# A triangular inverse on one NeuronCore: identity folded into its factors, the products copied by ScalarE, and the second token tile's products written to the other half of the partitions

## The reference, cut to what matters

```python
def gated_delta_rule(q, k, v, g, beta):          # 8 heads, chunks of 64 tokens
    ...
    a_mat = jnp.where(strict, jnp.einsum('nbhid,nbhjd->nbhij', kb, kc) * decay, 0.0)
    t_mat = a_mat + jnp.eye(CHUNK, dtype=jnp.float32)
    rhs = jnp.concatenate([vc * bc[..., None], kb * jnp.exp(gc)[..., None]], axis=-1)
    sol = lax.linalg.triangular_solve(t_mat, rhs, left_side=True, lower=True, unit_diagonal=True)
```

## Time and profile before

| what | value |
|---|---|
| time of three runs | median 2469.0 us (2468.1 to 2474.7) |
| the profiled execution | 2470.6 us, of which 2468.8 us are the span of the trace |
| TensorE | busy 2403.3 us, 97% of the span |
| VectorE | busy 1501.5 us, 61% |
| ScalarE | busy 1068.1 us, 43% |
| GpSimd | busy 151.8 us, 6% |

### The profile page before, as it was taken

One profiled execution on the slowest core, in us unless ns is written; L12 is line 12 of the kernel. 1 busy time (PEld: TensorE's weight loads), 2 busy tenths in 40 slices (PEclk: granted clock), 3 DMA queues, 4 the chain that ended last, 5 costly groups with the idle time before them and its releaser, 6 DMA issues. The chain is left out here.

```text
span 2468.8 us, 42893 instructions
## 1 busy us (share of the span) xinstructions
PE 2403.3 (97%) x18882; PEld 2222.7 (90%) x18882; DVE 1501.5 (61%) x2042; ACT 1068.1 (43%) x1319; POOL 151.8 (6%) x177
## 2 busy tenths in 40 slices
PE   8999999999999999999999999999998999999998
PEld 8999889999999799899889989899997998998997
DVE  5457664465567645667565556755676556866554
ACT  4334643333336543363343345533465335533432
POOL 0100000020000100001110000100001000111000
PEclk9999999999999999999999999999999999999999
DMA  6756355575564455543155554555545555423553
GB/s 228 241 188 155 107 175 184 186 226 190 185 165 128 151 187 186 158 139 104 53 196 188 188 156 137 171 188 188 178 137 171 188 188 162 121 87 103 181 188 118
DMA packets 320809, 405.37 MB, mean 164 GB/s; under 512 B 48688, under 2 KB 281232, under 8 KB 320624
## 3 DMA queue, kind: packets, MB, share of 16 engines
q1 hardware_dynamic: 314960, 383.50, 49.1%
q0 software_dynamic: 5664, 19.13, 2.5%
HBM read 401.55 MB, written 1.05 MB: 163 GB/s over the span
## 5 line engine op out<-in xcount | busy, mean ns | idle before, releaser
L402 DVE TENSOR_TENSOR w_lo<-raw,w_hi 128x2048 fp32r<-128x2048 f32 (+2 forms) x363 | 813.6, 2266 | 123.7 <-ACT w_hi L395 123.4
L395 ACT CAST w_hi<-raw 128x2048 fp32r<-128x2048 f32 (+2 forms) x363 | 685.5, 1890 | 462.5 <-PE ps L410 403.8
L408 PE MATMUL ps<-aT_hi,w_hi 128*128 128x256 f32 x2840 | 810.3, 285 | 0.0
L409 PE MATMUL ps<-aT_lo,w_hi 128*128 128x256 f32 x2840 | 804.4, 283 | 0.0
L410 PE MATMUL ps<-aT_hi,w_lo 128*128 128x256 f32 x2840 | 804.3, 283 | 0.0
L408 PEld LDWEIGHTS ps<-aT_hi,w_hi 128*128 128x128 f32 x2840 | 543.3, 191 | 7.0 <-issue 1.9
L409 PEld LDWEIGHTS ps<-aT_lo,w_hi 128*128 128x128 f32 x2840 | 543.5, 191 | 4.2 <-issue 0.5
L410 PEld LDWEIGHTS ps<-aT_hi,w_lo 128*128 128x128 f32 x2840 | 543.3, 191 | 0.5
L408 PE MATMUL ps<-w_hi,h_hi 128*128 128x512 f32 x928 | 363.6, 392 | 5.8 <-DVE h_lo L1758 4.6
L409 PE MATMUL ps<-w_lo,h_hi 128*128 128x512 f32 x928 | 362.6, 391 | 0.0
L410 PE MATMUL ps<-w_hi,h_lo 128*128 128x512 f32 x928 | 361.4, 389 | 0.0
(11 more groups left out here) (370 smaller groups left out, 1944.6 us busy)
## 6 DMA issues: line engine op xcount, KB each, us to landing
raw<-in_mlp_w SPq DMA_DIRECT2D x128, 1024.0 KB, 5.4
raw<-in_ffn_wd SPq DMA_DIRECT2D x44, 1024.0 KB, 4.9
raw<-in_ffn_wg SPq DMA_DIRECT2D x43, 1024.0 KB, 5.3
raw<-in_ffn_wu SPq DMA_DIRECT2D x43, 1024.0 KB, 5.3
raw<-in_gdn_w_in SPq DMA_DIRECT2D x32, 1024.0 KB, 5.7
raw<-in_mlstm_w_in SPq DMA_DIRECT2D x12, 1024.0 KB, 5.4
raw<-in_diff_w_in SPq DMA_DIRECT2D x12, 1024.0 KB, 5.3
raw<-in_w_in SPq DMA_DIRECT2D x8, 1024.0 KB, 5.2
```

Source lines behind the costliest of these rows:

```text
L395: nc.scalar.copy(used_part(hi_slot(n), n), used_part(raw[:, n % RAW, :], n)).then_inc(hi_ready, 1)
L402: nc.vector.tensor_tensor(used_part(lo_slot(n), n), used_part(raw[:, n % RAW, :], n), used_part(hi_slot(n), n).bitcast(F32), ALU.subtract) ...
L408: nc.tensor.matmul(dst, l_hi, r_hi, start=start, stop=False)
L409: nc.tensor.matmul(dst, l_hi, r_lo, start=False, stop=False)
```

## The change

The matrices are stored with the identity folded in: the masks of a level become "identity plus mask", and A becomes I - A, so that `right_set` yields I - Y, and the products T (I - Y) and (I - Y)T are the new T and its transpose without a subtraction. VectorE's `inverse_set` is gone; ScalarE copies the products from PSUM in `inverse_copied`. In `const_gdn` the diagonal is taken out of the chunk mask that spreads the row factors. `first_level` ends with a product by the mask in two halves for the second tile, since its transposed T is stored with the two chunks' partitions exchanged.

`blocks`, one call for each token tile, is replaced by `quarters`, one call for both: for each head it issues tile 0 chunk 0, tile 0 chunk 1, tile 1 chunk 0, tile 1 chunk 1. Where `over[t]` is set the output goes to the other half of the partitions. It is set for the second tile in `right`, in the first product of `both`, in the product by the identity at u = 10 and in the last level's second product; for levels 1 to 4 the second product of `both` has it unset for both tiles. One signal follows a call, and TensorE waits for both tiles ahead of it.

```diff
-    gdn = np.concatenate([same, np.where(col >= row, 0.0, NEG), row == col, level(0, col, row)]
-                         + [level(v, row, col) for v in range(1, LEVELS)], 1)
+    unit = (row == col).astype(np.float32)
+    gdn = np.concatenate([same & (s != t), np.where(col >= row, 0.0, NEG), unit, unit + level(0, col, row)]
+                         + [unit + level(v, row, col) for v in range(1, LEVELS)], 1)
...
-        def blocks(bank, lhs, rhs):
-
-            for h in range(HN):
-                for r in CK:
-                    last = nc.tensor.matmul(ps[r, bank, CHUNK * h:CHUNK * h + CHUNK], lhs[r, h, :], rhs(r, h), start=True, stop=True)
-            return last
...
+        def quarters(banks, lhs, rhs, over):
+
+
+            for h in range(HN):
+                for t in range(TT):
+                    for q, r in enumerate(CK):
+                        o = CK[1 - q] if over[t] else r
+                        last = nc.tensor.matmul(ps[o, banks[t], CHUNK * h:CHUNK * h + CHUNK], lhs[r, t, h, :], rhs(r, t, h),
+                                                start=True, stop=True)
+            return last
+
         def right(v):
             for t in range(TT):
                 if v == 1:
                     done(gd_T0, t)
                 else:
                     done(inv_t, TT * (v - 1) + t)
-                blocks(4 + t, g_A[:, t, :, :], lambda r, h: g_T[r, t, h, :]).then_inc(inv_y.sem, 1)
+            quarters((4, 5), g_A, lambda r, t, h: g_T[r, t, h, :], (0, 1)).then_inc(inv_y.sem, 1)
 
         def both(v):
             for t in range(TT):
                 done(inv_ys, TT * (v - 1) + t)
-                if v < LEVELS - 1:
-                    blocks(4 + t, g_TT[:, t, :, :], lambda r, h: g_Y[r, t, h, :])
-                blocks(6 + t, g_Y[:, t, :, :], lambda r, h: g_TT[r, t, h, :]).then_inc(inv_z.sem, 1)
+            if v < LEVELS - 1:
+                quarters((4, 5), g_TT, lambda r, t, h: g_Y[r, t, h, :], (0, 1))
+            quarters((6, 7), g_Y, lambda r, t, h: g_TT[r, t, h, :], (0, v == LEVELS - 1)).then_inc(inv_z.sem, 1)
...
             if u == 10:
                 for t in range(TT):
                     done(inv_t, t)
-                    blocks(4 + t, g_TT[:, t, :, :], lambda r, h: id64[r, :]).then_inc(inv_y.sem, 1)
+                quarters((4, 5), g_TT, lambda r, t, h: id64[r, :], (0, 1)).then_inc(inv_y.sem, 1)
...
+        def inverse_copied(v):
+            for t in range(TT):
+                done(inv_z, v - 1)
+                if v < LEVELS - 1:
+                    nc.scalar.copy(g_T[:, t, :, :], ps[:, 4 + t, :].rearrange("p (h c) -> p h c", c=CHUNK))
+                nc.scalar.copy(g_TT[:, t, :, :], ps[:, 6 + t, :].rearrange("p (h c) -> p h c", c=CHUNK)).then_inc(inv_t.sem, 1)
...
             if 3 <= u <= 14:
                 first_tap(u - 3, (u - 1) % 3)
+            if 10 <= u <= 14:
+                inverse_copied(u - 9)
...
-                m.append(ch.mark(nc.vector.tensor_tensor(g_TT[:, t, :, :], g_A[:, t, :, :], mask(level0T), ALU.mult)))
-            for t in range(TT):
-                ch.wait(m[2 * TT + t])
-                nc.vector.tensor_tensor(g_TT[:, t, :, :], mask(id64), g_TT[:, t, :, :], ALU.subtract).then_inc(inv_t.sem, 1)
+                m.append(ch.mark(nc.vector.tensor_tensor(g_A[:, t, :, :], mask(id64), g_A[:, t, :, :], ALU.subtract)))
+            ch.wait(m[2 * TT])
+            nc.vector.tensor_tensor(g_TT[:, 0, :, :], g_A[:, 0, :, :], mask(level0T), ALU.mult).then_inc(inv_t.sem, 1)
+            ch.wait(m[2 * TT + 1])
+            for r, o in (CK, CK[::-1]):
+                last = nc.vector.tensor_tensor(g_TT[o, 1, :, :], g_A[r, 1, :, :],
+                                               level0T[r, :].unsqueeze(1).to_broadcast([CHUNK, HN, CHUNK]), ALU.mult)
+            last.then_inc(inv_t.sem, 1)
...
-        def inverse_set(v):
-            for t in range(TT):
-                done(inv_z, TT * (v - 1) + t)
-                if v < LEVELS - 1:
-                    ch.mark(nc.vector.tensor_tensor(g_T[:, t, :, :], g_T[:, t, :, :], blocks(4 + t), ALU.subtract))
-                nc.vector.tensor_tensor(g_TT[:, t, :, :], g_TT[:, t, :, :], blocks(6 + t), ALU.subtract).then_inc(inv_t.sem, 1)
```

More of the change, by code:

```diff
@@ L2329, in two_block_model @@
     g_junk = ws[0][:, 0:D].rearrange("p (h v) -> p h v", v=P)
-    same_chunk = param[:, 0:P]
+    other_tokens = param[:, 0:P]
     g_upper, id64, level0T = (param[:, c:c + CHUNK] for c in (128, 192, 256))
@@ L2357, in two_block_model @@
     gd_T0 = gp("first_inverse_copied", TT)
-    inv_y, inv_ys, inv_z, inv_t = (gp("inverse_right", TT * LEVELS), gp("inverse_right_set", TT * (LEVELS - 1)),
-                                   gp("inverse_both", TT * (LEVELS - 1)), gp("inverse_set", TT * LEVELS))
+    inv_y, inv_ys, inv_z, inv_t = (gp("inverse_right", LEVELS), gp("inverse_right_set", TT * (LEVELS - 1)),
+                                   gp("inverse_both", LEVELS - 1), gp("inverse_set", TT * LEVELS))
     gd_kbe, gd_kst, gd_qe = gp("beta_k_decayed", TT), gp("state_keys", TT), gp("q_decayed", 4)
@@ L2585, in before @@
                         done(gd_kc, 3)
-                    nc.tensor.matmul(ps[:, 6 + t, :], same_chunk, ws[9][:, 512 * t:512 * t + 512], start=True, stop=True).then_inc(gd_brow.sem, 1)
+                    nc.tensor.matmul(ps[:, 6 + t, :], other_tokens, ws[9][:, 512 * t:512 * t + 512], start=True, stop=True).then_inc(gd_brow.sem, 1)
             if u == 10:
@@ L2786, in gdn_scalar @@
                 for t in range(TT):
-                    done(inv_y, t)
+                    done(inv_y, 0)
                     nc.scalar.copy(g_T[:, t, :, :], ps[:, 4 + t, :].rearrange("p (h c) -> p h c", c=CHUNK)).then_inc(gd_T0.sem, 1)
@@ L2895, in first_level @@
                 ch.wait(m[TT + t])
-                m.append(ch.mark(nc.vector.tensor_tensor(g_TT[:, t, :, :], g_A[:, t, :, :], mask(level0T), ALU.mult)))
-            for t in range(TT):
-                ch.wait(m[2 * TT + t])
-                nc.vector.tensor_tensor(g_TT[:, t, :, :], mask(id64), g_TT[:, t, :, :], ALU.subtract).then_inc(inv_t.sem, 1)
+                m.append(ch.mark(nc.vector.tensor_tensor(g_A[:, t, :, :], mask(id64), g_A[:, t, :, :], ALU.subtract)))
[6 more added lines that the diff above has]
+            last.then_inc(inv_t.sem, 1)
         def right_set(v):
             for t in range(TT):
-                done(inv_y, TT * v + t)
+                done(inv_y, v)
                 nc.vector.tensor_tensor(g_Y[:, t, :, :], blocks(4 + t), mask(levels[:, v - 1, :]), ALU.mult).then_inc(inv_ys.sem, 1)
-        def inverse_set(v):
-            for t in range(TT):
-                done(inv_z, TT * (v - 1) + t)
-                if v < LEVELS - 1:
-                    ch.mark(nc.vector.tensor_tensor(g_T[:, t, :, :], g_T[:, t, :, :], blocks(4 + t), ALU.subtract))
-                nc.vector.tensor_tensor(g_TT[:, t, :, :], g_TT[:, t, :, :], blocks(6 + t), ALU.subtract).then_inc(inv_t.sem, 1)
         def keys_decayed(t):
@@ L2990, in gdn_vector @@
                 first_level()
-            if 10 <= u <= 14:
-                inverse_set(u - 9)
             if 3 <= u <= 14:
```

## The result

The changed kernel takes 2450.3 us (median of four runs, 2448.3 to 2450.7) and the kernel before 2469.7 us beside it (four runs, 2468.1 to 2474.7). The ratio is 0.9919, with a 95% interval of 0.9907 to 0.9931. The forecast was 2448.6 us in a range of 2445 to 2461, and faster by more than 0.3% had a chance of 0.83.

What follows compares the result with a forecast made beforehand. TensorE, busy 2403.3 of 2468.8 us, was taken as the bound. From 2470.6 us profiled, less 20.6 for four quarters, plus 0.2 for `first_level`, came 2450.2; with the median 1.6 us lower, 2448.6 us, range 2445 to 2461.

Steps and rivals of the forecast that it cites:

- Four in turn, 14.6 ns a record: Mixers' small products: 704 of 960 records at 14.6 instead of 29.2 ns, saving 10.3 us a mixer, 20.6 both.
- The reasoning from pairs: In `quarters`: every pair among the four runs together today, each quarter at 58.4 ns, hence 14.6 ns a record.
- Rival 1: Small products: handing loads and matmuls to the array already sets 29 ns, four quarters bring nothing, 2469 us; chance 0.12.
- the estimate of 2463 us: Small products under the skill's 25 ns floor: 4.2 ns saved for each of 1,408 records, 5.9 us.
- Rival 2: Small products: only part of the four overlaps, say three; 19.5 ns a record, 13.7 us saved, 2455 us; chance 0.08.
- Rival 3: Small products: quarters sharing rows shut each other out; at worst 56 ns a record, 2507 us; chance 0.05.
- VectorE's subtractions at nothing: Mixer steps: removing VectorE's subtractions saves nothing, since they lay under the turned chunk and 24 matmuls.
- ScalarE's four copies: Behind `both` in each step: copies done after 2.2 us, 1.2 us of cover left before `right`, no cost on the path.
- Rival 4: Ahead of `right`: ScalarE's copies over 1.2 us late, each further microsecond costing 8 us; included in the forecast's range.
- One signal for a call: At `right_set`: the first tile starts up to one call later, with 1.6 us of cover left ahead of `both`.
- `first_level`'s further instruction: VectorE's third instruction there takes 0.6 us, delaying `right_set(1)`; counted 0.1 us a mixer, ends 0 and 0.6.
- The sum: Whole kernel: 2470.6 us profiled, less 20.6, plus 0.2, gives 2450.2; median 1.6 lower, so 2448.6 us.

Runs made afterwards that it cites:

- run 64: Not a follow-up run: "run" is a verb here, and 64 begins the product size 64 x 64 x 64; no kernel or time belongs to it.
- four-class kernel: The changed kernel with all of `both` in four quarters, tiles and head halves exchanged separately, A kept once more; medians 2444.3 and 2442.9 us, ratios 0.9900 and 0.9895.

## Why the prediction was right

- **Four in turn, 14.6 ns a record.** Right. The call measures 1.09 us (1.08 forecast), `both` 2.94 to 2.95 (2.9 to 3.0), the step 10.56 (10.56), the records 20.19 us (some 20). The kernel with opposite quarters only shows that this is the gain's cause, and the one with tile after tile that it needs the order too. The reasoning from pairs held: each quarter keeps the 58 ns a record that it has when two are in use, and the pairs that run together also run together as four.
- **Rival 1, issue as the bound.** Fell. Four records start within 20 ns, and 14.6 ns a record is kept over a whole call. The trace of the kernel before had already spoken against it: the single records of its calls start in pairs, 6 to 7 ns apart, and the next pair 58 ns after the first, so that 29 ns was only a mean and not a pace of issue. The prediction read the mean alone, and was wrong to say that this trace neither confirms nor refutes a floor of 25 ns from start to start. The Trainium skill's floor of about 25 ns from start to start ("TensorE: Matmul & The Clock Gate", section "Wait — 56ns, not 53.3ns?") does not hold across quarters of the array; the estimate of 2463 us worked out from it missed by 13.
- **Rival 2, only three overlap.** Fell with the same rows.
- **Rival 3, quarters that share rows exclude each other.** Fell: `both` would have become longer than 3.88 us and takes 2.94. The same page's rule ("Part 3: Packing small matmuls — row/col tiling") that a weight load overlaps matmuls only where the row groups differ is contradicted by this case: each record has a weight load of its own, and quarters of the same rows and other columns keep 58 ns a record each while all four run.
- **VectorE's subtractions at nothing.** Nearly right. With opposite quarters their removal is worth nothing (2453.7 against 2453.8 less the clock). Once the quarters shorten the step, they begin to count: kept, they hold up `both(2)` by 0.16 us, and by the mixers the kernel is 0.4 us slower for it (1.9 of its 2.3 us are the last level's second product, which is not in four quarters there).
- **ScalarE's four copies.** Right. They were done 2.16 us behind `both` (2.2 forecast), with 1.3 us of cover (1.2). Rival 4 did not come; the kernel with four copies more shows the edge where it would. The point from which it decides is about 1.2 us of ScalarE time a step, of which two more copies (0.96 us) take nearly all and cost nothing.
- **One signal for a call.** Right: no wait in the trace is put down to it, beyond the next point. No run takes it out alone.
- **`first_level`'s further instruction, 0.1 us a mixer.** Half right, too small. `both(1)` waits 0.13 us, as reckoned. But the instruction costs VectorE 0.9 us and not 0.6 (1114.38 to 1116.51 are 2.13 us where two instructions took 1.20: an instruction on 64 partitions takes 0.7 us, as long as one on 128), and the convolution behind it was late too: its lateness went over ScalarE's activation to the turned chunk, 0.2 us a mixer. The prediction asked only who waits for `right_set`; an instruction that is put ahead of a queue makes everything in it late.
- **The sum.** 2448.6 us was forecast and 2450.3 measured. The mixers gave 19.7 us of the 20.4 reckoned (20.6 less 0.2). Each gained 9.9: the 11 calls gave 11 x 0.93 = 10.2, and the two waits took 0.13 and 0.2. The other 1.0 us is within what the clock's stretches move from one execution to the next, and 0.7 of it is that the kernel before had its median at 2469.7 us beside the changed one, not at the 2469.0 from which the forecast started.

## What to carry to other kernels

Where small matmuls fill a quarter of the array, their cost is set by how many quarters have work at the same moment, so place outputs and operands so that four independent products fall in four different quarters, and write them in turn. An exchange of partition halves can be carried along, since each product may undo or keep it; here it cost no more than the further instruction in `first_level`, 0.33 us a mixer. To settle a few microseconds in a kernel whose clock drops now and then, compare distances between marks in the stretch that was changed and take the clock out of whole times; with VectorE's subtractions kept, the medians gave 13.7 us where the marks of an undisturbed execution gave 17.4.

## What the runs showed of the hardware

- Four quarters of TensorE run 64 x 64 x 64 float32 products at 14.6 ns a record, each quarter at 58 ns. Starts in different quarters lie 6 to 7 ns apart, at the seam of the tile-after-tile kernel 2 to 7.
- TensorE takes a record of an idle quarter ahead of earlier ones of busy quarters: by three records a quarter in the kernel with tile after tile, 0.17 us at the seam.
- In three traces of kernels with four quarters in turn TensorE idled in the middle of a call for nothing that the profile shows, 0.2 to 2.5 us: in the first mixer's `both(2)` each time after record 111, in the four-class kernel also in other calls (in the second mixer's `both(2)` after record 124). Each time it went on 2.2 to 2.6 us after the start of a 16 KB transfer of instructions. That the supply of instructions was the cause is read from this and not tested. The changed kernel's three profiled executions have no such gap in the mixers, nor have the two with more copies and the first run with VectorE's subtractions.
- The granted clock stood at 1.2 GHz for 25 to 48 us of an execution's span, at much the same places of the program, and once behind a stall of TensorE of 2.52 us. How often it falls differs from run to run, and with it much of the spread of one kernel's times: the four-class kernel's two profiled executions are 9.6 us apart in span and 20.6 us in time at the lower clock.
